# Three of the twelve modulation rows summed on VectorE instead of TensorE, in a two-block transformer kernel on one Trainium2 core

## The chip, the cores and the metric

The kernel runs on one core of one Trainium2 chip. The metric is the device time of one execution in microseconds; the median of three runs before the change is 2203.5 us (2201.97 to 2205.84).

## What is computed

The reference is two blocks of two layers each on 256 tokens of width 1024, all in float32. In each layer a vector of six modulation parts (shift, scale and gate, twice) comes from a conditioning vector. That product is what the change concerns:

```python
# first block, for each of two layers
c_act = jax.nn.silu(c)
mod = c_act @ w_ada[l] + b_ada[l]            # 1024 -> 6144
h = modulate(rms_norm(x, norm1_g[l]), sh1, sc1)
x = x + g1 * token_mixer(h, ...)             # gated linear attention + differential attention
x = x + g2 * hier_moe(modulate(rms_norm(x, norm2_g[l]), sh2, sc2), ...)
# second block, for each of two layers; the first layer also takes 256 context tokens
m = jax.nn.silu(cond) @ mod_w[i] + mod_b[i]  # cond is c_2, and c_ctx_2 for the context
y = attention_mixers(h, hc, ...)             # layer 0; layer 1 has a Fourier mix instead
x = x + g1 * rms_norm_2(y, norm_g[i, 1])
h = modulate_2(rms_norm_2(x, norm_g[i, 2]), sh2, sc2)
x = x + g2 * rms_norm_2(conv_ffn(h, ...), norm_g[i, 3])
```

## The kernel before

**Order of the work.** Every engine has a program of its own, written out by hand, and engines meet at semaphores. The stages in order of time: a prologue, mixer 0, the experts of layer 0 (MoE 0), mixer 1, MoE 1, then the attention of the second block: its heads (projections, head norms, rope; `pe_heads`, L2485, `dve_heads`), the attend loop (`pe_attend`, L2565), the output projection, the feed-forward network, and then the Fourier layer with its own. Nearly all loads of weights are issued by SyncE's one queue, in program order, each with a wait until its slot of SBUF is free.

**The modulation tiles.** The four products (two of the first block, n = 0 and 1, two of the second, n = 2 and 3) are cut into rows (n, r) with r = 0 to 2, each of 2048 outputs, and a row into eight tiles k of 128 inputs by 2048 outputs, 1 MB each: 96 tiles in all. Each is loaded by `sp_mods` (L673) through `load` (L338) into one of three slots (5, 6, 7), and multiplied by `pe_mods` (L694): four matmuls with the conditioning vector's 128 values, repeated to 32 columns, as the stationary operand (`crep`), each into its own 32 partitions of PSUM bank ps7, summed over k. After k = 7, VectorE copies the bank to `modrow` (L734), TensorE transposes that (`pe_mods_turn`, L690), and VectorE adds the bias and writes columns of `mods` (`dve_mods_turn`, L724). ps7 serves both the sums and the transposes, so the first tile of the next row waits until L724 has run. Some `pe_mods_turn` calls stand by themselves ahead of that tile, others happen inside `pe_mods` when k is 0.

**Where the tiles stand.** Tiles are put by hand between the other steps of TensorE's program: 8 in the prologue, 32 in each mixer (3 of those of mixer 1 in its first norm), 8 in the attention's heads and 16 in the attend loop. Row (2, 0) and all before it are needed before the second block begins, rows (2, 1) and (2, 2) after its attention and in its feed-forward network, row (3, 0) in the Fourier layer.

**The mixers.** `pe_mixer` (L1413) projects with `pe_fm` and `pe_tm`: each weight of 1 MB is split into a high and a low part in two units of half a weight; ScalarE writes the high part (L387, into one of four buffers HB), and GpSimd the low part (L393), and TensorE multiplies three times. Beside that, the gated linear attention goes through a chain: `pe_z` (log decays), VectorE and ScalarE (L1082, L1086, L1088, L1092, L1094), `pe_cum` (sums along the tokens), VectorE and ScalarE (L1115, L1119, L1126 to L1131), the keys' transposes (`pe_keys`, L1150), the states (`pe_states`). ScalarE makes the high parts of a later weight only after its part of this chain.

**The experts.** `sp_moe` (L1740) loads 192 MB of weights per layer, in order, over 13 or 14 slots, each as soon as TensorE has done with what was in it.

**The heads.** In `pe_heads` and `dve_heads` each of the projections q and k is copied from PSUM (L2403, L2432), two of the four of queries and two of keys are normed (`dve_hnorm`: a reciprocal, L2460, and a product, L2462), and six get the rotary embedding (`dve_rope`, three operations, L2477, L2478, L2480) after a matmul with a permutation. VectorE and TensorE alternate here. The attend loop waits for the last rope, `("roped", 3, 1)`, and on VectorE's side for `dve_units` (four times L393 for the output weights), which stands between the heads and the loop. The queue of SyncE loads four projection weights of the second block in this stretch (`sp_attention`, `sp_kv`), then those of the output, with modulation tiles between.

PSUM banks ps0 to ps3 (`bank`) are given out in turn, and a step waits until the bank's holder of four turns before is read.

## Time and profile before

| What | us |
|---|---|
| median of three runs | 2203.5 |
| lowest, highest run | 2201.97, 2205.84 |
| span of the profiled execution, first to last instruction | 2198.2 |
| TensorE busy in it (matmuls) | 2101.3 (96%) |
| VectorE busy | 986.7 (45%) |
| ScalarE busy | 711.6 (32%) |
| GpSimd busy | 285.1 (13%) |
| chain of waits: TensorE, DMA, VectorE | 81%, 10%, 5% |

The profile gives the span of the execution that it took, not that execution's own device time; the median of the runs is 5.3 us above the span, and it is taken here as span plus what lies around it. The chain of waits is followed back from the last instruction: TensorE's share of 81% is time in which a matmul, not something it waited for, was what the end depended on. PE is TensorE, DVE VectorE, ACT ScalarE, POOL GpSimd, SP SyncE. A busy share is an average: what a step costs has to be read in its own stage, where another engine may be the one that is waited for.

### The profile page before, as it was taken

The numbers are of one execution on the slowest core, as the hardware profiler recorded it, in microseconds if no ns is written. First come the engines' busy times: TensorE is split into PE (matmuls) and PEld (weight loads), VectorE is DVE, ScalarE is ACT, GpSimd is POOL, SyncE is SP. The second block draws the span as 40 slices with busy tenths as digits, with TensorE's granted clock in tenths as the row PEclk, the third lists the DMA queues.
The fourth block names the chain that finished last, engine by engine and source line by source line (L and its number), as shares of the span: only waits on it lengthen the run. The fifth ranks groups of instructions, "written<-read, shape, count | busy, mean of one in ns | idle before, by whom it ended". The sixth has DMA issues, their size and how long they took to land.

```text
span 2198.2 us, 30903 instructions
## 1 busy us (share of the span) xinstructions
PE 2101.3 (96%) x13133; PEld 1419.7 (65%) x13133; DVE 986.7 (45%) x1926; ACT 711.6 (32%) x1295; POOL 285.1 (13%) x145
## 2 busy tenths in 40 slices
PE   6999999999989989999999999899998999999999
PEld 3777784444434558877644444444764699978997
DVE  3465752222212237566322222221346587757776
ACT  3434431111101144454222111111213655566554
POOL 4554520000000035455000000000000000000000
PEclk8999999999999999999999999999999999999999
DMA  9965779999999997667799999999556285245550
GB/s 350 329 230 192 262 293 382 421 421 420 421 419 421 421 359 244 223 230 306 286 409 416 421 421 421 420 421 412 173 198 233 94 273 187 97 139 192 173 194 36
DMA packets 193594, 657.35 MB, mean 299 GB/s; under 512 B 12923, under 2 KB 116837, under 8 KB 131880
## 3 DMA queue, kind: packets, MB, share of 16 engines
q1 hardware_dynamic: 190784, 651.74, 76.4%
q8 instruction: 108, 1.77, 0.3%
q0 software_dynamic: 1184, 2.08, 0.3%
q10 hardware_dynamic: 1480, 1.45, 0.2%
q14 instruction: 38, 0.31, 0.0%
HBM read 654.17 MB, written 1.06 MB: 298 GB/s over the span
## 4 chain that ended last, share of the span: by engine, by line
PE 81%; DMA 10%; DVE 5%; ACT 2%; issue 1%; POOL 1%; SPq 0%; DVEq 0%; ACTq 0%; POOLq 0%
PE ps L410 79%; DMA ring<-in_w_expert_in 5%; DMA ring<-in_w_in 2%; DMA hT<-in_w_expert_in 1%; DMA HB<-in_w_expert_out 1%; DVE AR L762 1%; PE ps L2086 1%; DVE ARr L1687 0%; PE ps L2760 0%; PE ps L2582 0%; PE ps L1999 0%; POOL cols L522 0%; ACT HBr L387 0%; POOL wup L543 0%; DVE ringr L393 0%
## 5 line engine op out<-in xcount | busy, mean ns | idle before, releaser
L410 PE MATMUL ps<-ring,AR 128*64 128x512 f32 (+2 forms) x1952 | 531.3, 581 | 14.4 <-DMA ring<-in_w_expert_in 7.3
L410 PE MATMUL ps<-XLr,HBr 128*128 128x256 f32 x1280 | 371.7, 290 | 14.5 <-POOL ringr L393 5.0
L410 PE MATMUL ps<-hTr,ringr 128*128 128x256 f32 x1280 | 364.3, 285 | 0.0
L410 PE MATMUL ps<-hTr,HBr 128*128 128x256 f32 x1280 | 364.1, 284 | 0.0
L393 POOL TENSOR_TENSOR ringr<-ring,HBr 128x1024 fp32r<-128x1024 f32 x110 | 267.3, 2449 | 728.4 <-ACT HBr L387 728.2
L410 PEld LDWEIGHTS ps<-ring,AR 128*64 128x64 f32 (+1 forms) x1952 | 183.8, 142 | 271.1 <-issue 248.8
L410 PE MATMUL ps<-AR 128*128 128x128 f32 (+6 forms) x1928 | 327.8, 326 | 5.4 <-DVE AR L2030 2.8
L387 ACT ACTIVATE HBr<-ring 128x1024 fp32r<-128x1024 f32 x260 | 266.1, 1051 | 185.2 <-PE ps L410 161.4
L410 PEld LDWEIGHTS ps<-AR 128*128 128x128 f32 (+2 forms) x1928 | 218.8, 180 | 88.2 <-issue 66.7
L410 PEld LDWEIGHTS ps<-XLr,HBr 128*128 128x128 f32 x1280 | 247.7, 194 | 33.1 <-issue 18.0
L410 PEld LDWEIGHTS ps<-hTr,ringr 128*128 128x128 f32 x1280 | 247.9, 194 | 2.2 <-issue 1.2
L410 PEld LDWEIGHTS ps<-hTr,HBr 128*128 128x128 f32 x1280 | 247.6, 193 | 0.0
L393 DVE TENSOR_TENSOR ringr<-ring,HBr 128x1024 fp32r<-128x1024 f32 x150 | 179.2, 1223 | 76.6 <-ACT HBr L387 76.3
L2078 DVE SCALAR_TENSOR_TENSOR AR<-AR,ps 128x512 f32<-128x512 f32 x32 | 22.1, 690 | 374.5 <-ACT AR L2073 374.5
L410 PE MATMUL ps<-HB,AR 128*64 128x512 f32 x448 | 172.2, 593 | 0.5 <-DMA HB<-in_w_expert_out 0.5
L2073 ACT ACTIVATE AR<-ps 128x512 f32<-128x512 f32 x32 | 19.2, 599 | 436.7 <-PE ps L410 436.7
L2137 DVE SCALAR_TENSOR_TENSOR ARr<-ps,smal,ARr 128x512 fp32r<-128x512 f32 x64 | 45.2, 747 | 228.3 <-ACT ARr L2128 222.1
L410 PE MATMUL ps<-HBr,ARr 128*128 128x512 f32 x416 | 135.9, 395 | 0.0
L2128 ACT ACTIVATE ARr<-ps,smal 128x512 fp32r<-128x512 f32 x64 | 40.7, 685 | 207.6 <-PE ps L410 207.6
L410 PE MATMUL ps<-hT,AR 128*64 128x512 f32 x232 | 104.6, 593 | 1.2 <-DMA hT<-in_w_expert_in 1.2
L410 PE MATMUL ps<-XL,AR 128*64 128x512 f32 x232 | 104.7, 593 | 0.0
L410 PE MATMUL ps<-ring,crep 128*32 128x512 f32 x704 | 95.3, 621 | 4.9 <-DVE mods L724 4.3
(322 smaller groups left out, 2723.0 us busy)
## 6 DMA issues: line engine op xcount, KB each, us to landing
ring<-in_w_expert_in SPq DMA_DIRECT2D x151, 1024.0 KB, 20.2
ring<-in_w_expert_out SPq DMA_DIRECT2D x77, 1024.0 KB, 18.0
ring<-in_mod_w SPq DMA_DIRECT2D x48, 1024.0 KB, 6.7
ring<-in_ffn_w_up SPq DMA_DIRECT2D x44, 1024.0 KB, 5.2
ring<-in_w_in SPq DMA_DIRECT2D x40, 1024.0 KB, 5.8
ring<-in_w_ada SPq DMA_DIRECT2D x40, 1024.0 KB, 7.6
HB<-in_w_expert_in SPq DMA_DIRECT2D x33, 1024.0 KB, 21.6
HB<-in_w_expert_out SPq DMA_DIRECT2D x23, 1024.0 KB, 19.4
```

The source lines that it names most:

```text
L387: act.op.activation(hi, raw, ACT.Copy).then_inc(*act_hi.inc(*name))
L393: lane.op.tensor_tensor(lo, sel(chunk(of, k, w)), hi.bitcast(F32), ALU.subtract).then_inc(*count.inc(*name))
L410: return pe.op.matmul(out_, lhsT, rhs, start=start, stop=stop, **kw)
L762: dve.op.reciprocal(rs[:, 0:n], rs[:, 0:n]).then_inc(*dve_norm.inc(tag, "rstd"))
L2073: act.op.activation(m.th["th", l, p], bank["up", l, p, 0][:, :], ACT.Tanh, scale=0.5).then_inc(*act_moe.inc("th", l, p))
L2078: dve.op.scalar_tensor_tensor(t, t, 1.0, bank["up", l, p, 0][:, :], ALU.add, ALU.mult).then_inc(*dve_moe.inc("gated", l, p))
L2086: t = pe.op.transpose(bank["turn", l, p][:, k * 128:(k + 1) * 128], by_twos(m.th["th", l, p], k), ident)
L2128: act.op.activation(m.y["y", l, p][1][:, sl(half, 512)], bank["down", l, p, half][:, :], ACT.Copy, scale=m.gp["gp", l, p]).then_inc(*act_m ...
L2137: dve.op.scalar_tensor_tensor(yr[:, sl(2 + half, 512)], bank["down", l, p, half][:, :], m.gp["gp", l, p], yr[:, sl(half, 512)].bitcast(F32 ...
```

## The change

Rows (2, 1), (2, 2) and (3, 0) leave `pe_mods`. For each, VectorE multiplies tile 0 in its slot by the conditioning vector (one value per partition) and adds each further tile times its values in place (`dve_row_tiles`); TensorE then adds the 128 partitions of the sum with four matmuls by ones (`pe_row`), and VectorE copies the row (`dve_row_out`). These 24 tiles stand in the heads. The heads' 8 tiles on TensorE go, the attend loop keeps its 16, and each mixer has 8 tiles fewer on TensorE, at its first projections: 24 instead of 32. In `dve_mixer` the matching calls go. SyncE loads 16 tiles less in the mixers and 16 more around the heads; tiles from row (2, 1) on have four slots in turn (5, 6, 7 and 11) instead of three. The projection of the second keys and values (`pe_projkv(pe, 1, 0)`) moves ahead of one rope.

```diff
+        MODS_LATE = (5, 6, 7, 11)
...
+        ROWS_ON_DVE = ((2, 1), (2, 2), (3, 0))
...
+                    late = (n, r) > (2, 0)
+                    load(sp, ("mod", n, r, k), src.rearrange("p (o f) -> p o f", o=1), 1, 2048, MODS_LATE if late else MODS_IN)
...
+        def dve_row_tiles(dve, count):
+            for n, r, k in next_mods("rows", count):
+                name = ("mod", n, r, k)
+                w, c = mod_chunk(n, r, k), ctile[:, 8 * MODS[n][2] + k:8 * MODS[n][2] + k + 1]
+                dve.wait_ge(*landed(name))
+                if k == 0:
+                    dve.op.tensor_scalar(w, w, c, None, ALU.mult).then_inc(*dve_row.inc(*name))
+                else:
+                    before = ("mod", n, r, k - 1)
+                    dve.wait_ge(*dve_row[before])
+                    dve.op.scalar_tensor_tensor(w, w, c, mod_chunk(n, r, k - 1), ALU.mult, ALU.add).then_inc(*dve_row.inc(*name))
+                    slots.until(before, dve_row, *name)
+        def pe_row(pe, n, r):
+            b, name = ps[7], ("mod", n, r, 7)
+            pe_mods_turn(pe)
+            pe.wait_ge(*mbank.turn("sum", n, r))
+            pe.wait_ge(*dve_row[name])
+            w = mod_chunk(n, r, 7)
+            for j in range(4):
+                t = mm(pe, b[32 * j:32 * j + 32, :], C("ones", 0, 32), w[:, j * 512:(j + 1) * 512], True, True)
...
+        def dve_row_out(dve, n, r):
+            dve_mods_turn(dve)
+            dve.wait_ge(*pe_mod["mod", n, r, 7])
+            dve.op.tensor_copy(modrow, ps[7][:, :]).then_inc(*dve_mod.inc("row", n, r))
...
@@ sp_attention
             q_(0, 1)
-            sp_mods(sp, 1)
             q_(1, 0)
+            sp_mods(sp, 5)
+            q_(1, 1)
             sp_mods(sp, 2)
-            q_(1, 1)
             sp_kv(sp, 1)
+            sp_mods(sp, 5)
@@ pe_heads
-            pe_mods(pe, 2)
             pe_projq(pe, 0, 0, norm)
...
-            pe_mods(pe, 1)
             pe_rope(pe, m, 0, 0)
             pe_projq(pe, 1, 0, norm)
+            pe_row(pe, 2, 1)
             pe_hnorm(pe, m, 2, 0)
-            pe_mods(pe, 1)
             pe_rope(pe, m, 0, 1)
             pe_projq(pe, 1, 1, norm)
+            pe_mods_turn(pe)
             pe_hnorm(pe, m, 2, 1)
-            pe_mods(pe, 1)
             pe_rope(pe, m, 1, 0)
-            pe_mods(pe, 1)
+            pe_projkv(pe, 1, 0)
             pe_rope(pe, m, 2, 1)
-            pe_projkv(pe, 1, 0)
-            pe_mods(pe, 1)
+            pe_row(pe, 2, 2)
             pe_rope(pe, m, 1, 1)
             pe_projkv(pe, 1, 1)
-            pe_mods(pe, 1)
             pe_rope(pe, m, 3, 1)
+            pe_row(pe, 3, 0)
@@ dve_heads
-            norm.dve_apply(dve, 2)
+            norm.dve_apply(dve)
+            dve_row_tiles(dve, 3)
             dve_projq(dve, m, 0, 0)
+            dve_row_tiles(dve, 2)
             dve_projq(dve, m, 0, 1)
             dve_hnorm(dve, m, 0, 0)
+            dve_row_tiles(dve, 1)
             dve_projkv(dve, m, 0, 1)
             dve_hnorm(dve, m, 0, 1)
             dve_rope(dve, m, 0, 0)
+            dve_row_tiles(dve, 2)
             dve_projq(dve, m, 1, 0)
             dve_hnorm(dve, m, 2, 0)
+            dve_row_out(dve, 2, 1)
             dve_rope(dve, m, 0, 1)
+            dve_row_tiles(dve, 1)
             dve_projq(dve, m, 1, 1)
+            dve_mods_turn(dve)
             dve_hnorm(dve, m, 2, 1)
             dve_rope(dve, m, 1, 0)
+            dve_row_tiles(dve, 4)
+            dve_projkv(dve, m, 1, 0)
             dve_rope(dve, m, 2, 1)
+            dve_row_tiles(dve, 3)
+            dve_row_out(dve, 2, 2)
             dve_rope(dve, m, 1, 1)
+            dve_row_tiles(dve, 5)
             dve_projkv(dve, m, 1, 1)
+            dve_row_tiles(dve, 3)
             dve_rope(dve, m, 3, 1)
+            dve_row_out(dve, 3, 0)
@@ sp_program, after the experts of layer 1
-            sp_mods(sp, 2)
+            sp_mods(sp, 4)
             sp_attention(sp)
...
```

In `pe_mixer` the tiles go that stood after the first, second and third projection group, after `pe_z`, before `pe_cols`, after the projections `dproj` and the keys; in mixer 0 three stay, after the last three `dproj`, in mixer 1 none before `pe_dv`.

## Rows read from the trace of the kernel before

**Rows 1.** Windows by stage (window, length, busy PE, PEld, DVE, ACT, POOL, clock, DMA)
```profile
53.00:205.00 152.00, 148.19 (x1080) 117.33 (x1081) 82.14 (x126) 59.70 (x75) 76.86 (x33) 0.97 0.73 250
...
349.00:540.00 191.00, 191.00 (x1080) 93.69 (x1079) 43.59 (x117) 25.24 (x60) 0.00 (x0) 1.00 1.01 421
...
1539.00:1650.00 111.00, 106.79 (x508) 81.09 (x508) 43.47 (x58) 21.53 (x36) 0.00 (x0) 1.00 0.51 183
```

**Rows 2.** Modulation tiles on PE (ns min/median/max), and one between two ropes
```profile
L410 PE MATMUL ps<-ring,crep x704: 592/593/1063, 61.2 to 1708.6; 128*32 128x512 f32 x176
...
1588.03 1.06 PE L410 MATMUL ps<-ring,crep 128*32 128x512 f32 x8
1589.03 1.12 PE L410 MATMUL ps<-AR,cst 128*128 128x512 f32 x2
```

**Rows 3.** Timeline of mixer 0: VectorE's log decays, TensorE's sums and turned row
```profile
75.57 2.78 DVE L1094 TENSOR_SCALAR AR<-AR 128x1024 f32<-128x1024 f32 x1
...
79.02 2.05 PE L410 MATMUL ps<-cst,AR 128*128 128x128 f32 x16
...
83.26 0.23 PE L595 MATMUL ps<-cst,cols 10*128 10x10 f32 x1 [0.60 <-DVE cols L602]
...
89.39 1.06 PE L410 MATMUL ps<-ring,crep 128*32 128x512 f32 x8
...
99.80 0.66 PE L690 MATMUL ps<-cst,modrow 128*128 128x128 f32 x4 [0.23 <-DVE modrow L734]
102.18 1.90 PE L410 MATMUL ps<-ring,crep 128*32 128x512 f32 x8 [1.73 <-DVE mods L724]
```

**Rows 4.** Timeline of mixer 1: TensorE, GpSimd's low parts, VectorE's queries and copy
```profile
834.36 2.05 PE L410 MATMUL ps<-cst,AR 128*128 128x128 f32 x16
...
843.97 0.66 PE L690 MATMUL ps<-cst,modrow 128*128 128x128 f32 x4 [0.23 <-DVE modrow L734]
...
842.34 13.17 POOL L393 TENSOR_TENSOR ringr<-ring,HBr 128x1024 fp32r<-128x1024 f32 x5 [6.42 <-ACT HBr L387]
...
844.76 2.87 DVE L1141 TENSOR_TENSOR AR<-AR 128x512 f32<-128x512 f32 x1
...
858.91 0.68 DVE L1015 COPY AR<-ps 128x512 f32<-128x512 f32 x1
```

**Rows 5.** The DMA queue in the experts of layer 0: its waits, one issue
```profile
SPq L342 <- PE ps L410: 325.5, 99, 17.8
...
333.36 0.33 SPq L342 DMA_DIRECT2D XL<-in_w_expert_in  x1
```

**Rows 6.** VectorE in the attention's heads: two groups, and that window by engine
```profile
L2460 DVE RECIPROCAL AR<-AR 128x512 f32<-128x512 f32 x4 | 13.4, 3353 | 10.5 <-ACT AR L2449 10.5
...
L2462 DVE SCALAR_TENSOR_TENSOR AR<-AR,cols 128x512 f32<-128x512 f32 x4 | 3.0, 752 | 0.1
...
1556.10:1648.00 91.90, 88.23 (x412) 66.31 (x411) 36.83 (x43) 15.16 (x25) 0.00 (x0) 1.00 0.47 168
```

**Rows 7.** VectorE's timeline: length of its operations, and the attend loop's first
```profile
829.65 1.23 DVE L1092 SCALAR_TENSOR_TENSOR AR<-AR 128x1024 f32<-128x1024 f32 x1 [2.43 <-ACT AR L1088]
...
1652.12 0.69 DVE L2645 TENSOR_REDUCE smal<-ps 128x1 f32<-128x512 f32 x1
...
1655.41 0.49 DVE L2658 TENSOR_SCALAR AR<-AR,smal 128x512 f32<-128x512 f32 x1
```

**Rows 8.** DMA issues, 1535 to 1720 us: size, median us to landing
```profile
ring<-in_mod_w SPq DMA_DIRECT2D x22, 1024.0 KB, 5.1
```

**Rows 9.** TensorE after idle times (in brackets) about the heads, and its clock
```profile
1612.78 1.10 PE L410 MATMUL ps<-AR,cst 128*128 128x512 f32 x2 [2.00 <-DVE AR L2462]
...
1654.58 0.66 PE L2582 MATMUL ps<-cst,AR 128*128 128x128 f32 x4 [4.02 <-DVE AR L2658]
...
1655.00:1657.00 2.00, 2.00 (x8) 0.94 (x6) 1.02 (x5) 1.27 (x3) 0.00 (x0) 0.59 0.00 0
...
1614.00:1617.00 3.00, 3.00 (x16) 2.64 (x15) 2.57 (x4) 0.00 (x0) 0.00 (x0) 1.00 0.71 298
```

More of the change, by code:

```diff
@@ L653, in build @@
         MODS += [(A["mod_w_2"][l], f"mb{l}", 1, 96 + l * 48) for l in range(2)]
-        mod_items = [(n, r, k) for n in range(4) for r in range(3) for k in range(8)]
-        mod_at = {"sp": 0, "pe": 0, "dve": 0}
+        ROWS_ON_DVE = ((2, 1), (2, 2), (3, 0))
+        all_tiles = [(n, r, k) for n in range(4) for r in range(3) for k in range(8)]
+        row_tiles = [t for t in all_tiles if t[:2] in ROWS_ON_DVE]
+        mod_tiles = [t for t in all_tiles if t[:2] not in ROWS_ON_DVE]
+        mod_at = {"sp": 0, "pe": 0, "dve": 0, "rows": 0}
         mod_row = {"pe": None, "dve": None}
         def next_mods(lane, n):
+            tiles = {"sp": all_tiles, "rows": row_tiles}.get(lane, mod_tiles)
             a = mod_at[lane]
             mod_at[lane] += n
-            assert mod_at[lane] <= len(mod_items)
-            return mod_items[a:a + n]
+            assert mod_at[lane] <= len(tiles)
+            return tiles[a:a + n]
         def first_mod(n, r, k):
@@ L711, in pe_mods @@
                     mod_row["pe"] = n, r
+        def dve_row_tiles(dve, count):
[18 more added lines that the diff above has]
+                t = mm(pe, b[32 * j:32 * j + 32, :], C("ones", 0, 32), w[:, j * 512:(j + 1) * 512], True, True)
+            t.then_inc(*pe_mod.inc(*name))
+            slots.until(name, pe_mod, *name)
+            mbank.until(("sum", n, r), dve_mod, "row", n, r)
+            mod_row["pe"] = n, r
+        def dve_row_out(dve, n, r):
+            dve_mods_turn(dve)
+            dve.wait_ge(*pe_mod["mod", n, r, 7])
+            dve.op.tensor_copy(modrow, ps[7][:, :]).then_inc(*dve_mod.inc("row", n, r))
+            mod_row["dve"] = n, r
         def dve_mods_turn(dve):
```

80 lines of the change are left out of this document (29 added, 51 removed).

## The prediction, made before any run of the change

> **What bounds the kernel now.** I read the windows by stage first. Their columns after the length are busy time of matmuls, weight loads, VectorE, ScalarE and GpSimd, each with its count, then TensorE's clock as a share of full speed, the DMA engines' share and GB/s. TensorE is busy 148 of 152 us in the first half of mixer 0 and 107 of 111 us about the heads, so a matmul taken away there can shorten the kernel, unless it stood in for a wait; in the experts DMA runs at a share of 1.01 [rows 1]. A modulation tile on TensorE is eight matmul instructions (two for each float32 one), each 593 ns but four side by side; from the start of one tile to the next step is 1.00 us, and that is its price [rows 2]. In the heads VectorE is busy 36.8 of 91.9 us and idle 55.1 [rows 6]. The change takes 24 tiles from TensorE and puts their sums into that idle time.
>
> **Mixer 0: a gain of 9.** Eight tiles at 1.00 go: 8.0. A row is no longer turned after the second `dproj`: its transposes (99.80 to 100.46) and the wait for L724 (1.73) go, with 0.23 ahead, 2.6 in all, and the tile behind them, 1.90 long in place of 1.06, no longer runs at half the clock: 0.8 [rows 2, 3]. Against that, two waits grow. `pe_cum` at 79.02 needs L1094, which ends at 78.35 [rows 3]; that chain starts after `pe_z` (one tile earlier) and behind a high part that waits for the first half of v (two tiles earlier), so it moves by 2.0, while TensorE comes 4.0 earlier: 1.3 of them is waited away. At 83.26 TensorE already waits 0.60 for VectorE's copies [rows 3], so the tile ahead of them buys nothing: 1.0. The tile at 89.39 and those behind it come through, since GpSimd's low parts for the next weight move with the chain. 11.4 less 2.3 is 9.1.
>
> **Mixer 1: a gain of 4.** Here too eight tiles go, and the turn at 843.97 with its 0.23: 8.9 [rows 4]. But `pe_cum` again moves by 2.7 at most. The next weight's low parts are five in a row on GpSimd from 842.34, 13.17 long, so the first is ready at 845.0, just when its projection starts behind the turn, which ends at 844.6; they wait for ScalarE, which waits for the same chain, so this projection moves by 2.6 and not by the 5.9 taken away ahead of it. Next VectorE's queries, from 844.76 at 2.87 each beside GpSimd, start when the first keys are copied, some 3.7 earlier, and everything up to the copy at 858.91 that frees the states' bank moves by that [rows 4]. I take 3.9. Both mixers: 13, between 9 (if the new waits of 1.3 to 2.2 us also cost clock) and 20.3 (all of it).
>
> **Experts and loads: nothing.** A saturated DMA might swallow the gain of mixer 0. But in the experts of layer 0 the queue waits for TensorE 99 times, 325.5 us in all, and the loads that fill DMA start at 333.36, released by a matmul [rows 5]. They start as much earlier as TensorE does. The mixers' 16 loads fewer are covered by TensorE's work, where the DMA share is 0.73 [rows 1]; if a transfer were late there, the change would gain by it. The last tile sits in another slot than before, under 0.5 us either way.
>
> **Heads: a loss of 20.** TensorE: 8 tiles less 3 rows of four matmuls at the same 1.00 each would be 5 us saved. VectorE: an operation with two float32 tensors takes 1.23 us at 1024 columns (829.65) and 0.75 at 512 [rows 6, 7], so about 2.37 at 2048, plus 0.04 to a dependent one; a tensor_scalar takes 0.49 at 512, about 1.3 at 2048 [rows 7]. 21 x 2.41 + 3 x 1.34 = 54.6, plus two row copies more at 0.69: 56 us against 55.1 idle [rows 6]. It would need every gap, and some can't be used. I went through `pe_heads` and `dve_heads` in their new order with these prices and the waits of the code:
> - 3 tiles end at 1565.7, 2 more at 1571.2, one at 1580.1: no delay. The first projection gains 0.8 only, since its two tiles covered the norm.
> - VectorE then has nothing to do until the second head norm's root: the reciprocal starts at 1588.2 (before: 1588.86, after 7.79 idle of the 10.5 of its group [rows 6]). No tile stands there: 7.5 us lost.
> - Norm, rope and 2 tiles end at 1599.3. TensorE has been ready for row (2, 1) since 1595.3: it waits 4.0.
> - Third norm (waits 2.2), row copy, rope, a tile, copy, fourth norm, rope: 1617.9. 4 tiles, copy, rope, 3 tiles: 1637.6. Row (2, 2) waits 11 us on TensorE, then VectorE 1.2 for its result.
> - Rope, 5 tiles, copy, 3 tiles, last rope: 1663.2. Row (3, 0) needs L724 of row (2, 2), which stands behind that rope: sum and copy add 2.1. With the 4.6 of `dve_units` the attend loop starts on VectorE at 1669.9.
>
> Before it was 1652.12 [rows 7]; the same walk over the old order gives 1653.1, so the loss is 16.8. A load lands 5.1 us after its issue [rows 8], taken as 5.2 with four slots; it delays a tile by 0.5 twice. The Trainium skill (DMA: Bandwidth & Descriptors, section Measured) has 6.15 us for 1 MB; by that estimate the loss would be 2.6 more. The rows have the same thing shorter, and I go by them.
>
> **The clock.** After an idle of 4.02 at 1654.58 TensorE runs at 0.59 of its clock in the next window (near 1.2 GHz instead of 2.4), after one of 2.00 at 1612.78 at 1.00 [rows 9]. The new waits are 4.0, 11 and 7.9 us, all on steps that VectorE waits for next; with 3 us of half speed behind each (an estimate: the window of 0.59 starts 0.4 us after the wait and is 2 us long [rows 9]) the walk ends 4.0 us later. Bounds: 16.8 and 20.8; I take 20, near the upper, since 4.02 is the row most like the new waits. Without any clock loss the sum below would be 2207. The Trainium skill (TensorE: Matmul & The Clock Gate, section HAM oscillation) tells that a kernel which waits in each turn of its loop pays a slow start each time; by that the three waits cost what I add, and the rows of 4.02 and 2.00 agree with it for the longer wait alone.
>
> **Attend loop and later: 0.** Its 16 tiles stay; the turn of row (3, 0) moves from its first step to its second. The four projection weights now queue behind tiles on SyncE: the last two, behind a tile slot that comes free at 1599.3, land near 1607 to 1609, and are needed at 1612 to 1619. If they were late by a landing, 5 us.
>
> **Sum.** -9.1 - 3.9 + 20 = +7. Against the execution's span of 2198.2 that is 2205.2, and with the 5.3 by which the median lies above the span, 2210.5. A measurement can tell about 0.2% (4.4 us) from no change, so this is slower by a little more than that.
>
> **Rivals.**
> 1. *Nearly even* (0.19): mixers 15, heads 17. For it: each term is within 3 of its estimate, and the two nearly cancel. 2205, within 0.2%.
> 2. *The mixers give all they lose* (0.17): 20.3, because the chains move as TensorE does, with heads at 16.8: -3.5, 2200, and down to 2197 with a cheaper wait. For it: every tile stood on a busy TensorE [rows 1]. Against: the zero slack in [rows 3, 4]. This is the case on the other side; it decides as soon as the mixers' gain exceeds the heads' loss by 4.4.
> 3. *VectorE's sums hide* (0.06): 54.6 do fit into 55.1 in sum [rows 6]. Heads -5, mixers -13 to -20: 2178 to 2185. Against: the 7.5 us without a tile and the alternation.
> 4. *The experts swallow the mixers' gain* (0.08): if the saturated loads were set by DMA and not by TensorE [rows 5], only the heads' 20 remain: 2223.
> My forecast, between 2208 and 2218, has 0.50.
>
> The change does cut TensorE's tiles; that it might not is no real case here.
>
> **Range and chances.** 2197 to 2219 leaves out rivals 3 and 4 and some tail, 0.18 together. Slower by over 0.2%: 0.50 + 0.08 = 0.58. Within: 0.19 and 0.05 of rival 2, 0.24. Faster: 0.12 + 0.06 = 0.18.
>
> **What would show it.** Right: in the heads VectorE nearly without idle time but for one gap of 7 us before the second reciprocal; row matmuls after waits of 4, 11 and 8 us on VectorE's tile sums; the attend loop starting some 20 us later after the last expert than before; 21 sums of 2.3 us; mixer 0 shorter by 9, mixer 1 by 4, with a new wait of over 1 us at `pe_cum` in both. Wrong: sums near 1.2 us, tiles late by DMA for more than 2 us in all, mixers shorter by over 17, or experts that start earlier and end no earlier.

## The result, and the profile after

| | before | after |
|---|---|---|
| median, us | 2202.7 | 2223.7 |
| lowest, highest of 4 runs | 2199.31, 2205.84 | 2218.08, 2225.24 |
| span of the profiled execution | 2198.2 | 2223.4 |

The ratio is 1.0087, with a 95% interval of 1.0076 to 1.0099: slower by 21 us by the medians, by 19 by the ratio. The forecast was 2210.5, and 2197 to 2219 its range; the sign was right, the size was not. The profiled execution of the kernel after took 2225.24 us and was the slowest of its four; the one before, with 2198.2, is short for its kernel, so the two traces lie 25 us apart.

The cores view of the kernel before and of the one after, then from the page of the latter the busy time of each engine and the chain of waits:

```profile
core 0: 2198.2 us, clock 0.989
...
core 0: 2223.4 us, clock 0.977
...
PE 2096.7 (94%) x12965; PEld 1429.9 (64%) x12965; DVE 1044.0 (47%) x1950; ACT 711.5 (32%) x1295; POOL 286.5 (13%) x145
...
PE 76%; DMA 10%; DVE 9%; ACT 2%; issue 1%; POOL 1%; SPq 0%; DVEq 0%; ACTq 0%; POOLq 0%
```

TensorE is only 4.6 us less busy, although 24 tiles of some 1.00 us went and three rows of 1.9 came. Its mean clock was 0.989 before and is 0.977: of the 2223 us about 102 were at half speed (1.2 GHz of 2.4), in place of 48 (twice the missing share of the span). The last line is the chain of waits: VectorE's share rose from 5% to 9%.

To see where the time went, I took the start of the same matmul in both traces and subtracted. The difference goes to -10.7 us in mixer 0, stays there through the experts, rises by 6.3 in mixer 1 and by 22.0 in the heads, and by some 7 in the first feed-forward network (FFN).

The heads of the kernel after. First the stage by windows (columns as in [rows 1]: length, busy PE, PEld, DVE, ACT, POOL, clock, DMA share, GB/s), from the same point on to the attend loop:

```profile
1535.00:1668.00 133.00, 108.32 (x472) 83.38 (x473) 96.38 (x86) 21.52 (x36) 0.00 (x0) 0.89 0.72 272
...
1620.00:1650.00 30.00, 19.05 (x74) 13.65 (x73) 25.70 (x18) 0.60 (x1) 0.00 (x0) 0.77 0.99 385
```

Before it was 111 us long with 43.47 of VectorE at clock 1.00 [rows 1]. In its 30 us from 1620 TensorE is busy 19, VectorE 25.7, the clock is 0.77 and DMA is full.

The waits of TensorE in that stage, grouped (engine line waited for: us in total, times, longest), then the three row matmuls in the timeline (start, length, idle time in brackets), and the longest idle time of VectorE:

```profile
PE ps L411 <- DVE biasB L730: 15.0, 2, 11.0
PE ps L411 <- DVE mods L764: 7.5, 1, 7.5
```

```profile
1595.70 1.94 PE L411 MATMUL ps<-biasB,cst 128*32 128x512 f32 x8 [4.05 <-DVE biasB L730]
...
1635.88 1.94 PE L411 MATMUL ps<-biasB,cst 128*32 128x512 f32 x8 [10.95 <-DVE biasB L730]
...
1663.52 1.93 PE L411 MATMUL ps<-biasB,cst 128*32 128x512 f32 x8 [7.53 <-DVE mods L764]
```

```profile
1584.65 3.35 DVE L2485 RECIPROCAL AR<-AR 128x512 f32<-128x512 f32 x1 [7.67 <-ACT AR L2474]
...
1670.67 0.68 DVE L2675 TENSOR_REDUCE smal<-ps 128x1 f32<-128x512 f32 x1
```

The row matmuls take 1.94 and not 1.06: TensorE is at half clock when it comes out of each wait. The attend loop starts on VectorE at 1670.67, before at 1652.12 [rows 7]. The sums in the same stretch, by form:

```profile
L730 DVE SCALAR_TENSOR_TENSOR ring<-ring,smal 128x2048 f32<-128x2048 f32 x12 | 28.2, 2349 | 1.3 <-DMA ring<-in_mod_w 0.6
...
L726 DVE TENSOR_SCALAR ring<-ring,smal 128x2048 f32<-128x2048 f32 x3 | 3.8, 1280 | 0.0
```

Mixer 0 and mixer 1, TensorE's new waits in the timeline. The first two lines answer to [rows 3], the others to [rows 4]; the last group is VectorE, with the last step of the queries, the decay factors and the copy for which TensorE waits:

```profile
75.88 2.02 PE L411 MATMUL ps<-cst,AR 128*128 128x128 f32 x16 [1.55 <-DVE AR L1128]
...
80.09 0.23 PE L596 MATMUL ps<-cst,cols 10*128 10x10 f32 x1 [1.07 <-DVE cols L603]
...
846.53 0.79 PE L411 MATMUL ps<-AR 64*128 64x256 f32 x1 [3.63 <-DVE AR L1049]
```

```profile
838.05 2.90 DVE L1177 TENSOR_TENSOR AR<-AR 128x512 f32<-128x512 f32 x1
...
842.07 1.19 DVE L1309 TENSOR_TENSOR AR<-lamv 128x64 f32<-128x64 f32 x1
843.18 2.38 DVE L1310 TENSOR_TENSOR AR<-lamv 128x64 f32<-128x64 f32 x1
...
845.80 0.68 DVE L1049 COPY AR<-ps 128x512 f32<-128x512 f32 x1
```

GpSimd's low parts in the kernel after at this place, and in the kernel before the two decay factors with the last low part beside them:

```profile
829.54 15.94 POOL L394 TENSOR_TENSOR ringr<-ring,HBr 128x1024 fp32r<-128x1024 f32 x6 [5.87 <-ACT HBr L388]
```

```profile
856.06 2.40 POOL L393 TENSOR_TENSOR ringr<-ring,HBr 128x1024 fp32r<-128x1024 f32 x1 [0.55 <-ACT HBr L387]
...
857.18 1.36 DVE L1275 TENSOR_TENSOR AR<-lamv 128x64 f32<-128x64 f32 x1
858.46 0.21 DVE L1276 TENSOR_TENSOR AR<-lamv 128x64 f32<-128x64 f32 x1
```

And the FFN, which no edit touches: the issue of its first four loads on SyncE's queue (start, and the time from the first issue of the group to the last), a stretch of the chain of waits, and one of TensorE's new waits:

```profile
1720.51 55.20 SPq L343 DMA_DIRECT2D ring<-in_ffn_w_up  x4
```

```profile
1775.34 5.17 DMA ring<-in_ffn_w_up
1780.53 1.07 ACT HBr L388
1781.62 1.23 DVE ringr L394
```

```profile
1788.26 0.36 PE L411 MATMUL ps<-XLr,HBr 128*128 128x256 f32 x1 [2.22 <-DVE ringr L394]
```

Before, the same four loads stood 19.48 us in the queue:

```profile
1705.02 19.48 SPq L342 DMA_DIRECT2D ring<-in_ffn_w_up  x4
```

In the kernel after the last one is issued at 1775 and lands 5.17 later, with everything behind it waiting.

### The profile page after: what moved, and what is told of

It reads as the page before. It is cut to its first block, busy times and chain, and to the rows that moved or that the text cites. A ratio compares the mean times of both kernels' runs of the same rounds, so it can differ in the third digit from the quotient of the medians.

```text
span 2223.4 us, 30613 instructions
## 1 busy us (share of the span) xinstructions
PE 2096.7 (94%) x12965; PEld 1429.9 (64%) x12965; DVE 1044.0 (47%) x1950; ACT 711.5 (32%) x1295; POOL 286.5 (13%) x145
## 3 DMA queue, kind: packets, MB, share of 16 engines
q0 software_dynamic: 1184, 2.08, 0.3%
HBM read 654.17 MB, written 1.06 MB: 295 GB/s over the span
## 4 chain that ended last, share of the span: by engine, by line
PE 76%; DMA 10%; DVE 9%; ACT 2%; issue 1%; POOL 1%; SPq 0%; DVEq 0%; ACTq 0%; POOLq 0%
PE ps L411 74%; DMA ring<-in_w_expert_in 5%; DMA ring<-in_w_in 2%; DMA hT<-in_w_expert_in 1%; DMA HB<-in_w_expert_out 1%; DVE AR L802 1%; DVE ring L730 1%; DVE ringr L394 1%; PE ps L2110 1%; ACT HBr L388 1%; DMA ring<-in_mod_w 0%; DVE ARr L1711 0%; DVE biasB L730 0%; PE ps L2791 0%; DVE AR L2485 0%
## 5 line engine op out<-in xcount | busy, mean ns | idle before, releaser
L411 PE MATMUL ps<-AR 128*128 128x128 f32 (+6 forms) x1928 | 335.0, 330 | 6.8 <-DVE AR L1049 3.6
L411 PEld LDWEIGHTS ps<-AR 128*128 128x128 f32 (+2 forms) x1928 | 223.6, 183 | 89.6 <-issue 69.7
L411 PE MATMUL ps<-ringr,ARr 128*128 128x512 f32 x240 | 94.9, 395 | 0.9 <-DVE XLr L943 0.9
## 6 DMA issues: line engine op xcount, KB each, us to landing
HB<-in_w_expert_in SPq DMA_DIRECT2D x33, 1024.0 KB, 20.4
```

The source lines that it names most:

```text
L411: return pe.op.matmul(out_, lhsT, rhs, start=start, stop=stop, **kw)
```

## Where each kernel won and lost

All times of a stage below are differences to the profiled execution of the kernel before, in us: how much later than there the matmul at the stage's end starts, less the same at its beginning. The boundaries lie at 125, 815, 1120, 1555, 1700 and 2190 us of the kernel before; mixer 0 is taken with the prologue, the heads with the attend loop's beginning, and "from there" is all the rest. It is one execution each, and stages that no edit touches differ by up to 3 us between executions.

| kernel | mixer 0 | experts 0 | mixer 1 | experts 1 | heads | from there | ratio of the runs (95%) |
|---|---|---|---|---|---|---|---|
| after | -10.7 | -0.3 | +6.3 | +1.0 | +22.0 | +6.8 | 1.0087 (1.0076-1.0099) |
| ffn_slots | -9.1 | +1.2 | -0.4 | +1.1 | +23.7 | +0.3 | 1.0053 (1.0040-1.0067) |
| ffn_slots_again | -9.7 | +1.0 | +0.8 | -0.1 | +21.3 | +0.1 | 1.0050 (1.0032-1.0068) |
| before_slots | -0.2 | +1.3 | +1.5 | +1.3 | 0.0 | -0.1 | 1.0002 (0.9992-1.0012) |
| before_slots2 | -0.9 | -0.2 | +2.0 | +1.2 | 0.0 | +6.9 | 1.0032 (1.0021-1.0043) |
| short_sums | -10.3 | -0.3 | +1.1 | -0.5 | +10.0 | +8.4 | 1.0024 (1.0014-1.0034) |
| short_loads | -10.0 | +1.3 | +0.8 | -0.4 | +21.3 | -0.1 | 1.0040 (1.0027-1.0053) |
| short_both | -10.1 | +1.2 | +0.7 | +0.5 | -0.9 | 0.0 | 0.9957 (0.9944-0.9971) |
| gap_tiles | -9.1 | +3.4 | -0.7 | -0.6 | +14.4 | -0.1 | 1.0021 (1.0012-1.0030) |
| fill_heads | -10.1 | -0.2 | +1.0 | -0.1 | +30.0 | +0.3 | 1.0081 (1.0066-1.0096) |
| fill_two | -10.8 | -0.1 | +1.0 | -0.2 | +20.4 | 0.0 | 1.0035 (1.0023-1.0047) |
| lambda_later | -9.8 | +1.3 | -2.9 | +0.3 | +20.1 | +6.5 | 1.0072 (1.0059-1.0085) |
| fill_wait | -10.5 | +2.4 | -1.4 | +0.8 | +23.1 | 0.0 | 1.0027 (1.0012-1.0043) |
| fill_more | -9.1 | +2.2 | -2.9 | +0.5 | +23.5 | 0.0 | 1.0031 (1.0022-1.0041) |
| two_rows | -9.7 | +2.1 | +1.6 | -1.8 | +0.6 | +0.2 | 0.9960 (0.9946-0.9974) |
| two_rows_b | -10.3 | +3.2 | +1.6 | -0.4 | +2.4 | +0.2 | 0.9959 (0.9945-0.9973) |

`before_slots` turned out to be the kernel before with other names, so its row shows the scatter of the method; its mixer 1 and its experts together lie 4 us behind the execution that the forecast was made against, which was a short one: the time of a run is 1.8 to 1.9 us above its span, so that execution took some 2200 us where the medians are 2202 to 2204.

## Experiments on the FFN

**ffn_slots**: the kernel after, with the FFN's first loads starting at slot 6, as before the change.

```diff
+        FFN_IN = (6, 7, 5)
@@ sp_ffn
-                among = MODS_IN if g == 0 else ALL
+                among = FFN_IN if g == 0 else ALL
@@ sp_fourier
-            load(sp, ("dft",), by_rows(A["dft"]), 2, 2 * NF, MODS_IN)
+            load(sp, ("dft",), by_rows(A["dft"]), 2, 2 * NF, FFN_IN)
```

> The kernel after, with one edit: the first loads of the FFN (up of its first quarter) and dft take their slots in the order 6, 7, 5, in a rotation of their own, so that they start at slot 6 as they did before the change. Theory (slot rotation: 24 modulation loads fewer shifted the rotation, so that the second half of up got slot 5, which the first half's neighbour still held): the four issues of up on SyncE wait for about 20 us again and not for 55, the waits of 5.17 us on DMA and of 1.8 and 2.2 us on VectorE between 1775 and 1790 us go, the FFN is shorter by 6.5 us and the kernel comes to 2217 us (ratio to before 1.0058). Rival (the FFN lost its time to the clock or to a tile of the attend loop): the issues come early, and less than 2 us are gained, 2222 or more.

Measured: 2216.61, ratio 1.0053. The issues of the first four loads take 19.48 us again, and the waits of 1.83 and 2.22 are gone:

```profile
1721.49 19.48 SPq L344 DMA_DIRECT2D ring<-in_ffn_w_up  x4
```

The theory holds: 7 us for a rotation of slots, with the same bytes and the same work. The count makes it plain. 88 tiles went through slots 5, 6 and 7 before the FFN, 48 after (the rest has the turn of four); 88 leaves 1 and 48 leaves 0 when divided by 3. So the two halves of the FFN's first weight went to slots 6 and 7 before and go to 5 and 6 now, and the second half of the next weight, whose slots are 4 and 5 both times, must wait until TensorE has used the first.

**before_slots** was to make the same collision in the kernel before, by `FFN_IN = (5, 6, 7)`.

> The kernel before, with one edit: up of the FFN's first quarter takes slots 5, 6, 7 in a rotation of its own, starting at 5. In the kernel before its halves went to 6 and 7 of the three. No modulation tile is touched. Theory (slot rotation): if slots 5 and 6 give the same collision as in the kernel after, the FFN loses 6 to 7 us here too, 2209 us, ratio 1.003. Rival: the collision needs the late end of the attend loop's tiles of the kernel after as well; then less than 1 us is lost, ratio 1.000.

Measured: 2202.60, ratio 1.0002. This says nothing on either theory: the rotation is counted per tuple of slots, and (5, 6, 7) is the tuple of the modulation tiles, so no load had changed its slot (19.48 us of issues, as before).

**before_slots2** is the same with `FFN_IN = (5, 6, 7, 5, 6, 7)`, a tuple with a count of its own.

> The kernel before, with one edit: the FFN's first loads and dft have a rotation of their own over slots 5, 6, 7 that starts at 5 (in the earlier run of that kind the rotation was still shared with the modulation tiles, so the slots were those of before and nothing had changed). No modulation tile moves. Theory (slot rotation): the four issues of up take 55 us instead of 19, since the last of them needs slot 5, which the first half of up holds until TensorE has used it; the FFN loses 6 to 8 us, 2209 us, ratio 1.003. Rival (the issues come late and the load still lands in time, because the kernel before reaches the FFN with nothing late): under 1 us, ratio 1.000.

Measured: 2210.36, ratio 1.0032, and +6.9 in the trace at the FFN. The lines are those of the kernel after, the issues and TensorE's waits on VectorE's low parts:

```profile
1711.28 48.67 SPq L343 DMA_DIRECT2D ring<-in_ffn_w_up  x4
```

```profile
1767.04 0.38 PE L411 MATMUL ps<-XLr,HBr 128*128 128x256 f32 x1 [1.73 <-DVE ringr L394]
...
1772.40 0.36 PE L411 MATMUL ps<-XLr,HBr 128*128 128x256 f32 x1 [2.23 <-DVE ringr L394]
```

One edit takes the loss out of the kernel after and another puts it into the kernel before, with no tile moved. That settles 7 of the 21 us. All further variants of the kernel after start at slot 6, but for `lambda_later` and `short_sums`; the base of the others is `ffn_slots`.

## Experiments on the heads

**short_sums**: what do VectorE's sums cost? Only 64 columns are summed.

```diff
-                    dve.op.tensor_scalar(w, w, c, None, ALU.mult)...
+                    dve.op.tensor_scalar(w[:, 0:64], w[:, 0:64], c, None, ALU.mult)...
-                    dve.op.scalar_tensor_tensor(w, w, c, mod_chunk(n, r, k - 1), ALU.mult, ALU.add)...
+                    dve.op.scalar_tensor_tensor(w[:, 0:64], w[:, 0:64], c, mod_chunk(n, r, k - 1)[:, 0:64], ALU.mult, ALU.add)...
```

> The kernel after, with the sums of the three late rows made over 64 of the 2048 columns only, so the rest of these rows is left out; all instructions, waits, loads and matmuls stay. Theory (VectorE's time for the sums makes the heads longer): the waits of 4.0, 11.0 and 7.5 us of TensorE on the row sums vanish, the half clock behind them too, and the heads come to between -5 and +1 us against the kernel before instead of +22; kernel 2200 to 2206 us, ratio 1.000. Rival (the tiles' loads or the row matmuls and their turn cost as well): the waits stay in part, on DMA, and the heads are still over 4 us longer than before; 2207 to 2212.

Measured: 2208.71, ratio 1.0024. The rival was right. With the sums all but free, the heads still cost 10.0 us, since VectorE now waits for the tiles. (The FFN's collision, +8.4 in this execution, is in the 1.0024 as well.) Its waits, grouped, and the stretch by windows:

```profile
DVE ring L730 <- DMA ring<-in_mod_w: 17.5, 6, 6.0
...
DVE biasB L730 <- DMA biasB<-in_mod_w: 5.7, 3, 2.2
```

```profile
1620.00:1650.00 30.00, 21.59 (x87) 15.21 (x86) 9.80 (x20) 5.66 (x6) 0.00 (x0) 0.86 1.02 414
```

23.2 us of waits on DMA in place of the 1.0 of the kernel after, at a DMA share of 1.02. This second bound stands right behind VectorE's.

**short_loads** is the counterpart: whole sums, and of each tile only 64 columns loaded.

```diff
+                    if (n, r) in ROWS_ON_DVE:
+                        name = ("mod", n, r, k)
+                        sp.wait_ge(*slots.turn(*name, among=MODS_LATE))
+                        s = slots[name]
+                        sp.op.dma_start(slot_at[s][0][:, 0:64], src[:, 0:64]).then_inc(*slot_in[s].inc(*name))
...
```

> The kernel after with the FFN's first loads at slot 6 (2216.6 us measured); of the 24 tiles that VectorE sums only 64 of the 2048 columns are loaded, so the rest of those rows is left out. The sums keep their full size and all waits stay. It is the counterpart of the run with short sums, in which VectorE waited 23 us for the tiles and the heads still cost 10 us. Theory (VectorE's sums alone give nearly the whole price, the loads stand just behind them): the waits of 4, 11 and 8 to 9 us stay within 1.5 us, the heads cost 18 to 22 us, kernel 2212 to 2217. Rival (the loads give half of the price): the heads cost 10 to 13 us, 2203 to 2207.

Measured: 2212.17, ratio 1.0040; heads +21.3, against 23.7 and 21.3 in the two executions of its base. The DMA share from 1620 to 1650 fell to 0.26 and the waits stayed:

```profile
1591.12 1.94 PE L412 MATMUL ps<-biasB,cst 128*32 128x512 f32 x8 [4.05 <-DVE biasB L737]
...
1631.04 1.94 PE L412 MATMUL ps<-biasB,cst 128*32 128x512 f32 x8 [10.89 <-DVE biasB L737]
...
1657.88 1.94 PE L412 MATMUL ps<-biasB,cst 128*32 128x512 f32 x8 [6.79 <-DVE mods L771]
```

So VectorE sets the heads of the kernel after, as forecast, and the loads would give half of the price if it did not.

**short_both** closes the square.

> The kernel after with the FFN's first loads at slot 6; of the 24 tiles that VectorE sums only 64 of 2048 columns are loaded and summed, the rest of those rows is left out. It closes the square: heads against the kernel before with both whole +23.7, with short sums +10.0, with short loads +21.3 us. Theory (sums and loads are all that the heads lose by; the order and the row matmuls cost nothing): the heads come to -6 to -3 us, kernel 2187 to 2191. Rival (the new order of ropes, projections and row matmuls costs by itself): the heads at 0 to +6, 2193 to 2199.

Measured: 2193.19, ratio 0.9957; heads -0.9, between the theory (-6 to -3) and the rival (0 to +6). The order costs a few us by itself. TensorE waits 3.17 at row (2, 2), 1.75 at row (3, 0) and 4.46 at the start of the attend loop:

```profile
1617.47 1.07 PE L412 MATMUL ps<-biasB,cst 128*32 128x512 f32 x8 [3.17 <-DVE biasB L737]
...
1636.45 1.07 PE L412 MATMUL ps<-biasB,cst 128*32 128x512 f32 x8 [1.75 <-DVE mods L771]
```

The heads in the four corners: whole sums and loads +21.3 to +23.7, loads only +10.0, sums only +21.3, neither -0.9. The two costs lie beside each other and don't add. It also bounds what three rows can give in this order: with sums and loads both all but free, the kernel is 9 us below the one before (2193.19 against 2202.27) and no more. The row matmul behind the wait of 3.17 took 1.07 and so ran at full clock.

**gap_tiles**: the forecast had found 7.5 us in which VectorE has no tile to sum. Here two tiles stand there.

```diff
             dve_projkv(dve, m, 0, 1)
+            dve_row_tiles(dve, 2)
             dve_hnorm(dve, m, 0, 1)
             dve_rope(dve, m, 0, 0)
-            dve_row_tiles(dve, 2)
```

> The kernel after with the FFN's first loads at slot 6 (2216.6 us measured) and one edit: the two sums that stood behind the first rope now stand ahead of the second head norm, where VectorE had 7.7 us of idle time. Theory (VectorE's order is what binds in the first half of the heads): the wait of 4.0 us at the row (2, 1) goes, every later wait starts some 4.8 us earlier, and 5 to 6.5 us are gained: 2210 to 2212 us. Rival (the loads bind in the second half of the heads, where the DMA share was 1.00 over 30 us): the wait at row (2, 1) goes, VectorE then waits for tiles (DMA) by as much, and 0 to 2 us are gained: 2215 to 2217.

Measured: 2207.44, ratio 1.0021, against 1.0053 and 1.0050 in the two runs of its base: 6 to 7 us less, and 7 to 9 less in the heads of the traces, at the theory's upper end or above it. VectorE's idle time before the reciprocal is 2.95 instead of 7.67, the first wait is gone, and with it a part of the half clock (0.96 from 1590 to 1620, after 0.89 and 0.94 in the base):

```profile
1581.33 3.35 DVE L2486 RECIPROCAL AR<-AR 128x512 f32<-128x512 f32 x1 [2.95 <-ACT AR L2475]
```

The rival, loads that bind, fails here: VectorE waits 1.0 us for tiles. For three rows on VectorE the placement of two sums alone was some third of the price of the heads.

**fill_heads**: does TensorE's clock matter in the heads? Matmuls of no use, 3, 9 and 6 of them, ahead of the three waits.

```diff
+            for _ in range(fill):
+                mm(pe, b[:, :], C("ones"), cst[:, 0:512], True, True)
             pe.wait_ge(*dve_row[name])
```

> The kernel after with the FFN's first loads at slot 6 (2216.6 us measured) and matmuls of no use (all-ones by a constant, 128x512) in the bank of the row sums ahead of each of the three waits on VectorE: 3, 9 and 6 of them, at 1.13 us each less than the waits of 4.0, 10.9 and 9.0 us. Theory (about 6 of the 23 us that the heads cost are TensorE at half clock behind these waits): the windows of 0.77 and 0.89 come to 0.95 or more, the waits shrink to about 1 to 3 us each, and 4 to 7 us are gained: 2210 to 2213. Rival (the half clock lies beside waits on VectorE and costs little): 0 to 2 us, 2215 to 2217.

Measured: 2220.70, ratio 1.0081, slower than its base. The third fill was misplaced: it stands behind the wait for the columns of row (2, 2), 9.61 us, and then ran for 8.3 us on the path.

```profile
1657.06 8.31 PE L412 MATMUL ps<-cst 128*128 128x512 f32 x12 [9.61 <-DVE mods L767]
```

**fill_two** leaves that one out. **ffn_slots_again** is the base beside it.

> As the run with fills in the heads, without the third fill: that one stood behind the wait for the last columns of row (2, 2) and so ran after the wait of 9.6 us, on the path, for 8.3 us. Here 3 and 9 matmuls of no use stand in the waits at rows (2, 1) and (2, 2) only. Base: the kernel after with the FFN's first loads at slot 6, run again beside this one. Theory (the half clock behind these two waits costs about what was forecast for all three, 2 to 3 us): granted clock 0.94 or more from 1590 to 1650, 2 to 3 us less than the base, where the earlier run had gained 2.1 at the last row's wait before its third fill. Rival (VectorE is the chain, TensorE's clock in the heads does not matter): 0 to 1 us.

> The same kernel as ffn_slots (the kernel after with the FFN's first loads at slot 6), as the base beside the two runs with fills, since the run with 3 fills in mixer 1 came out 6 us below the first run of this base, in another group, and the trace shows 2.4. If the base comes to 1.0050 or more of the kernel before again, fills in mixer 1 gain something that the trace of one execution doesn't show; if it comes to 1.003 to 1.004, the difference was scatter between groups of runs.

Measured: 2211.65 and 2214.19, ratios 1.0035 (1.0023 to 1.0047) and 1.0050 (1.0032 to 1.0068). In the trace the heads are 0.9 us shorter than in the one execution of the base and 3.3 than in the other. The windows from 1590 to 1620 and to 1650, base first:

```profile
1590.00:1620.00 30.00, 28.41 (x118) 21.23 (x118) 24.93 (x20) 2.49 (x4) 0.00 (x0) 0.94 0.65 241
1620.00:1650.00 30.00, 19.28 (x76) 14.40 (x77) 25.18 (x19) 0.32 (x1) 0.00 (x0) 0.77 1.00 393
```

```profile
1590.00:1620.00 30.00, 30.00 (x124) 22.54 (x121) 26.90 (x23) 2.49 (x4) 0.00 (x0) 1.00 0.73 274
1620.00:1650.00 30.00, 22.77 (x89) 15.74 (x87) 24.91 (x15) 5.64 (x6) 0.00 (x0) 0.92 0.99 384
```

The clock rises as expected; the gain is 1 to 3 us and the intervals overlap, so theory and rival aren't told apart. The base itself came out at 1.0050 again.

## Experiments on mixer 1

**lambda_later**: in mixer 1 the copy for which TensorE waits 3.63 us goes ahead of the decay factors.

```diff
-            dve_lambda(dve, l, m)
+            if l == 0:
+                dve_lambda(dve, l, m)
             dve_dproj(dve, l, m, 1, 0)
+            if l == 1:
+                dve_lambda(dve, l, m)
```

> The kernel after, with one edit: in mixer 1 VectorE copies the first half of the projected deltas out of the projection's bank before it computes the decay factors (3.57 us in two operations), which stood ahead. Theory (the new wait of 3.63 us of TensorE ahead of the states comes from VectorE's queue, and the half clock in the 6.8 us behind it costs 2.4 us more): the wait falls to under 0.6 us, the granted clock stays at 1.00 there, and mixer 1 is shorter by 3 to 6 us; kernel 2218 to 2221. Rival 1 (the decay factors are needed just as early by the next step): the wait moves behind the states and 0 to 1 us is gained, 2223. Rival 2 (the low clock is not tied to that wait): the wait goes and its 3 us are gained, and the half clock stays.

Measured: 2218.95, ratio 1.0072 against 1.0087 (intervals overlap); mixer 1 -2.9. The wait did not go: it stands a few matmuls later, for the next copy behind the decay factors.

```profile
849.00 1.22 PE L411 MATMUL ps<-AR,cst 128*128 128x512 f32 x1 [2.96 <-DVE AR L1212]
```

The mixer lies 2 to 4 us below the other executions of the kernel after's mixer 1 (-0.7 to +1.1), near the theory's lower end, while the wait behaved as rival 1 said. The two matmuls behind it took 2.08 together, at half clock, though this idle time is shorter than the 3.17 of `short_both`. The kernel still has the FFN's collision (+6.5).

**fill_wait**: 3 matmuls of no use ahead of that copy's wait.

```diff
+            else:
+                pe_busy(pe, hbank, 3, "fill", l)
             pe_states(pe, l, m, 0)
```

> The kernel after with the FFN's first loads at slot 6 (2216.6 us measured) and 3 matmuls of no use (1.13 us each) ahead of the states of mixer 1, in the wait of 3.63 us on VectorE's copy. Theory (in mixer 1 the chain by VectorE moved by 3 us as the copies did, and 1.5 to 2.9 us of that go to the clock behind the new wait): the idle time falls under 0.6 us, the granted clock between 847 and 861 us is 1.00, TensorE stands 2.5 to 3 us earlier against the kernel before at the end of this stretch than at its beginning, where the five executions of the same code so far had 0 to 1.5; kernel 2214.5 to 2216. Rival (the gain is lost to something else than the clock): the clock is 1.00 and the gain stays at 0 to 1.5.

Measured: 2210.30, ratio 1.0027. The fills took less than I had priced, 1.15 us of idle time were left, and the clock behind it was 0.88 from 847 to 861, as in one execution of the base. In that stretch, then, nothing had changed, and the time was 4 to 6 us below the base. The interval (1.0012 to 1.0043) touches that of the second base run (1.0032 to 1.0068). The profiled execution, 2214.42, was the slowest of the six, 4.1 above their median, so the trace can't show what the median gained; why this kernel is faster stays open.

**fill_more**: 4 in place of 3.

> As the run with 3 fills ahead of the states of mixer 1, with 4: 3 took 2.5 us there (6 instructions at 0.41) and left 1.15 us of the wait, and the stretch behind it was at half clock as before. Base: the kernel after with the FFN's first loads at slot 6, run again beside this one. Theory A (the half clock behind the copy follows from the idle time): with under 0.4 us idle the clock between 847 and 857 is 1.00 and 1.7 us are gained there. Theory B (it comes from elsewhere, from the sparse matmuls of the states, of which 8 to 13 run in 3.4 us): the clock stays at 0.5 to 0.6 in the window behind the copy and nothing is gained.

Measured: 2211.71, ratio 1.0031 beside the base's 1.0050. The idle time is 0.30, and the windows from 847 to 861, base first, then this kernel, read:

```profile
847.00:861.00 14.00, 12.13 (x61) 9.77 (x62) 9.73 (x17) 3.21 (x4) 3.13 (x2) 0.76 0.17 50
```

```profile
847.00:861.00 14.00, 13.70 (x78) 9.82 (x77) 12.54 (x21) 3.46 (x5) 4.61 (x3) 1.00 0.35 108
```

From 815 to 870 us this kernel gains 3.1 on the kernel before, the two executions of the base 1.5 and 0.2. Theory A holds, theory B falls: the half clock behind the copy follows from the idle time, and costs 1.6 to 2.9 us. The same matmuls of the states run at full clock when TensorE was not idle before them; all nine executions with the wait of 3.63 us left whole have a clock of 0.76 to 0.88 there. By the runs, `fill_wait` and `fill_more` (1.0027 and 1.0031) lie about 5 us below the two runs of the base (1.0053 and 1.0050), more than this stretch accounts for. The Trainium skill (TensorE: Matmul & The Clock Gate, section HAM oscillation) describes a kernel whose work behind each wait starts slow; the trace agrees, and adds that work of no use in the wait takes the slow start away.

## Two rows instead of three

**two_rows** keeps what paid: mixer 0 of the kernel after, mixer 1 of the kernel before, 16 sums in the heads with three of them in the gap, and the FFN's slots. The first lines below are against the kernel after, those of the heads on VectorE against the kernel before:

```diff
-        ROWS_ON_DVE = ((2, 1), (2, 2), (3, 0))
+        ROWS_ON_DVE = ((2, 2), (3, 0))
@@ dve_heads: 3 tiles before projq(0,0), 2 before projq(0,1), then
             dve_projkv(dve, m, 0, 1)
+            dve_row_tiles(dve, 3)
             dve_hnorm(dve, m, 0, 1)
             dve_rope(dve, m, 0, 0)
+            dve_row_out(dve, 2, 2)
...
             dve_rope(dve, m, 2, 1)
+            dve_row_tiles(dve, 2)
             dve_projkv(dve, m, 1, 0)
+            dve_row_tiles(dve, 3)
             dve_rope(dve, m, 1, 1)
+            dve_row_tiles(dve, 2)
             dve_projkv(dve, m, 1, 1)
+            dve_row_tiles(dve, 1)
+            dve_row_out(dve, 3, 0)
             dve_rope(dve, m, 3, 1)
```

> Only two rows, (2, 2) and (3, 0), go to VectorE. Mixer 0 is that of the kernel after (24 tiles), mixer 1 and its order that of the kernel before (32 tiles), the heads have 16 sums in place of 24: 3 and 2 ahead of the first two projections' copies, 3 in the gap ahead of the second head norm's root where the kernel after has none, 2, 3, 2 and 1 from the last second rope on; the last row's matmul stands ahead of the last rope, and the FFN's first loads start at slot 6. Theory (in mixer 0 the tiles pay about 9, in mixer 1 nothing; 24 tiles are too many for VectorE and for the loads in the heads, 16 fit both: 16 sums of 2.4 us are 38 of 55 us idle): mixer 0 -8 to -10, mixer 1 0, heads between -5 and +3, FFN 0: 2187 to 2198 us, ratio 0.993 to 0.998. Rival (each row on VectorE costs the heads its share of the 22 us, by its order and not by its number): heads +10 to +15, kernel 2203 to 2209.

Measured: 2193.12, ratio 0.9960 (0.9946 to 0.9974): 9.5 us faster than the kernel before and 28 to 31 faster than the one after. Heads +0.6, mixer 0 -9.7. It changes the number of rows, their order and mixer 1 at once, so what each of them gave isn't separated. The page's first part, and TensorE's waits in the heads:

```profile
PE 2091.4 (95%) x13021; PEld 1421.4 (65%) x13021; DVE 1023.8 (47%) x1942; ACT 711.1 (32%) x1295; POOL 285.7 (13%) x145
```

```profile
PE ps L412 <- DVE AR L2492: 4.2, 1, 4.2
PE ps L2612 <- DVE AR L2688: 4.0, 1, 4.0
PE ps L412 <- DVE AR L2510: 1.7, 1, 1.7
```

No wait on a sum is left. The second and third waits are those that the kernel before has at the same places (4.02 [rows 9] and 1.67); the first, at the rope behind the fourth norm, was 2.00 there [rows 9].

**two_rows_b** puts the matmul of row (2, 2) into that wait, and its copy and turn behind the ropes.

> The kernel with two rows on VectorE (2193.1 us measured) and one step moved: the matmul of row (2, 2) from behind the first rope to the wait of 4.18 us on VectorE's fourth norm, its copy and turn behind the ropes. Theory: the matmul's 1.0 us lies in a wait, that wait falls to 3.1, and the half clock behind it (0.89 in this stretch) goes as it did before behind waits of 2: 1 to 3 us gained, 2190 to 2192. Rival (slot held longer by the row, a tile of the last row late): 0 or a loss of 1 to 2 us.

Measured: 2194.23, ratio 0.9959, no difference. The wait fell from 4.18 to 2.99, but the row (3, 0), 2.36 us late on its sum, took the microsecond back. The half clock did not go either: the two matmuls behind the wait took 2.04 in both kernels, where they take 1.10 in the kernel before [rows 9]. The rival holds.

## Why the forecast was right in its sign and short in its size

- **Mixer 0, -9.1 forecast: right.** -9.1 to -10.7 in all executions of that code, with the new waits nearly as priced: 1.55 at `pe_cum` (forecast 1.3) and 0.46 and 1.07 at the columns, where 0.60 was before (forecast 1.0 more).
- **Experts, 0: nearly right.** Those of layer 0 came out at -0.3 to +3.4, where two more executions of the kernel before had +1.3 and -0.2; those of layer 1 at -1.8 to +1.1. Rival 4, that they swallow all 9, did not happen.
- **Mixer 1, -3.9: wrong, by 2 to 5, by the execution of the kernel before that one takes.** The sum had the chain right: the copy that TensorE waits for comes 13.1 us earlier (858.91 to 845.80) where the mixer began 11.0 earlier, so 2.1 are gained, less than the 3.7 that the queries should have given. The last microseconds of the chain went to the decay factors, which took 1.19 and 2.38 us beside GpSimd's low parts; in the kernel before they took 1.36 and 0.21, the second from 858.46 on, just when GpSimd's low part of 2.40 us had ended. The forecast had no wait at this place, and so no clock for it: the 3.63 us of idle time bring half clock behind them, 1.6 to 2.9 us (fill_more). The stage came out at -0.7 to +1.1 in eight executions of this code and at +6.3 in the profiled one of the kernel after, which had more stretches of half clock (at 908, 1027 and 1061 us). From 804 to 1122 us its clock is 0.96, and 0.98 in both profiled executions of the base; that is 13 us more at half clock, an estimate from these means, and would account for 6 us. Why they fall there in one execution and not in the next isn't shown. Other executions of the mixer of the kernel before came out at +1.5 to +2.0, so what the 8 tiles gave is 2 us at most. For both mixers that is the lower bound of 9 that the forecast had named.
- **Heads, +20: right within 1.3 to 3.7.** The waits of 4.0, 11 and 7.9 came as 4.05, 10.95 and 7.53, the gap of 7.5 as 7.67, the sums at 2.35 (forecast 2.37) and 1.28 (1.3). Tiles came late by 1.0 us. With the walk's 16.8 that leaves 3.5 to 6 us, for which the forecast had 4.0 of half clock. The trace has much of it (clock 0.77 for 60 us), but the fills show only that 1 to 3 us hang on the first two waits; how much of the rest is clock isn't shown. Half clock on an engine that would wait anyway costs little.
- **Attend loop and later, 0: the step that failed.** "Its 16 tiles stay", and I had looked for late weights of the output projection, not for what 40 loads fewer in a rotation of three do to the loads behind them. The remainder changed, and the FFN lost 7 us. That is the main miss: without it the kernel stands at 2214 to 2217, inside the range, and still slower than the kernel before (1.0050 and 1.0053), so the sign was no luck.
- **Rivals.** Rival 3 (the sums hide) would not have been reached even with free sums: the loads hold 10 us. Rival 2 needed 20 from the mixers; they gave 9 to 10. Rival 4's time, 2223, is the one that was measured, but by chance: the experts did not swallow the mixers' gain.
- **Sum.** Mixers and experts about -8, heads +22, FFN +7: +21 against the execution of 2198.2. The three profiled executions with the work of the kernel before lie 2 us behind it on average in mixers and experts (0, +2.1 and +3.9), which leaves +19; the runs gave 19 by the ratio (17 to 22).

## What to carry to other kernels

Where buffers go round by a counter, count what each pass leaves: loads taken out of one stage shift the slots of every later one, and a collision can cost as much as the whole change. When work moves to an idle engine, price it by the order of that engine's program and not by its idle sum, and ask which bound stands next (here the loads, 10 us behind VectorE's 21). Take work away only up to the first wait that it uncovers: 8 tiles in mixer 0 paid 9 us, the 8 in mixer 1 at most 2, and with 16 sums the heads were as long as before (+0.6 and +2.4) where with 24 they were 22 longer, or 14 with two sums better placed.

## What the runs showed of the hardware

- VectorE beside GpSimd: a TENSOR_TENSOR of 128x64 took 2.38 us in place of 0.21, one of 128x512 2.90, while GpSimd's low parts ran (each some 2.5 us). The 2.38 ended at 845.56, GpSimd's stretch at 845.48. Even the smallest operation of this kind can take as long as one of GpSimd's beside it.
- Idle times of 3.63 us on TensorE were followed by half clock, 0.76 and 0.88 over 14 us in two executions of one kernel; with 0.30 us the clock was 1.00, with 1.15 it was 0.88. The length of the idle time alone doesn't decide: behind 2.96 us (lambda_later) and 2.99 (two_rows_b) the clock was half, behind 3.17 (short_both) it was full. The Trainium skill (TensorE: Matmul & The Clock Gate, section Part 1: The HAM clock gate) notes that the number of slow matmuls at a kernel's start changes from run to run of one kernel. The rows here show such a change in the middle of a kernel, and it makes a single execution a poor measure of a stage: to within 3 us, and 7 in mixer 1 (-0.7 to +6.3).
- The loads of the heads alone can hold DMA at a share of 1.02 and 414 GB/s for 30 us (short_sums), and at 0.99 while VectorE is the one that is waited for (after): a share near 1 doesn't tell which of the two binds, the waits by releaser do.
